# Every second panel of the last up GEMM as three fp32r passes, with low parts made by accumulating transfers

## The reference

```python
def conv_ffn(h, w_up, conv_w, conv_b, w_down, rows):
    u = h @ w_up
    if rows is None:
        u = dwconv1d(u, conv_w[1], conv_b)
    else:
        u = dwconv2d_grid(u, conv_w, conv_b, rows)
    a, g = jnp.split(u, 2, axis=-1)
    return (jax.nn.silu(g) * a) @ w_down
```

## Time and profile before

| | before |
|---|---|
| median of 3 runs | 2967.87 us |
| the profiled execution, its own time | 2972.56 us |
| its span | 2970.5 us |
| TensorE matmul busy | 2742.2 us (92%) |
| VectorE busy | 1932.8 us (65%) |
| ScalarE busy | 1088.4 us (37%) |
| GpSimd busy | 183.0 us (6%) |
| mean granted TensorE clock | 0.973 |

### The profile page before, as it was taken

The page is one execution under the profiler, slowest core; times in us unless marked ns, Lnnn a source line. Parts: engine busy times, 40 slices in busy tenths (PEclk is TensorE's granted clock), DMA queues, the critical chain, the costliest instruction groups (busy, mean ns, idle before and its releaser), DMA issues.

```text
span 2970.5 us, 48700 instructions
## 1 busy us (share of the span) xinstructions
PE 2742.2 (92%) x18394; PEld 2327.1 (78%) x18394; DVE 1932.8 (65%) x3303; ACT 1088.4 (37%) x1387; POOL 183.0 (6%) x85
## 2 busy tenths in 40 slices
PE   3999998999999998999989958999999899889998
PEld 3998977899999887899967844687744777668887
DVE  6776665677777765466756373577786676664881
ACT  2434432443542424154463542333300644442211
POOL 0000000000000000000022300244300000000000
PEclk9999999999999999999999979999999999999999
DMA  8775734577675543446412010122277221113441
GB/s 305 271 286 217 267 114 165 211 278 283 216 273 218 213 169 115 158 141 227 183 57 74 30 64 29 67 89 99 106 264 288 73 73 69 57 57 122 149 166 73
DMA packets 105950, 469.13 MB, mean 158 GB/s; under 512 B 7004, under 2 KB 56744, under 8 KB 57896
## 3 DMA queue, kind: packets, MB, share of 16 engines
q1 hardware_dynamic: 105768, 466.67, 43.3%
HBM read 465.58 MB, written 1.06 MB: 157 GB/s over the span
## 4 chain that ended last, share of the span: by engine, by line
PE 35%; DVE 10%; DVEq 7%; ACT 3%; issue 3%; DMA 1%; ACTq 1%; SPq 0%
PE accs L826 6%; DVEq L2818 4%; PE accs L687 4%; PE accs L688 4%; PE accs L689 4%; PE accs L672 4%; DVE arena L2795 3%; PE accs L1215 2%; PE accs L1216 2%; PE accs L1217 2%; DMA arena<-wc 1%; PE accs L1348 1%; ACT arena L76 1%; PE mix L1272 1%; DVE arena L2103 1%
## 5 line engine op out<-in xcount | busy, mean ns | idle before, releaser
L687 PE MATMUL accs<-normed_r,arena_r 128*128 128x256 f32 (+2 forms) x1864 | 586.4, 315 | 14.6 <-DVEq L2148 6.3
L689 PE MATMUL accs<-normed_r,panel_r 128*128 128x256 f32 (+2 forms) x1872 | 585.7, 313 | 0.0
L688 PE MATMUL accs<-arena_r 128*128 128x256 f32 x2069 | 584.5, 282 | 0.0
L86 DVE TENSOR_TENSOR panel_r<-panel,arena_r 128x1024 fp32r<-128x1024 f32 (+1 forms) x295 | 387.2, 1312 | 162.4 <-ACTq L1468 117.1
L1467 ACT ACTIVATE arena_r<-panel 128x1024 fp32r<-128x1024 f32 (+1 forms) x292 | 330.4, 1132 | 330.4 <-DMA panel<-w 140.8
L687 PEld LDWEIGHTS accs<-normed_r,arena_r 128*128 128x128 f32 (+1 forms) x1864 | 350.9, 188 | 51.8 <-issue 12.7
L688 PEld LDWEIGHTS accs<-arena_r 128*128 128x128 f32 x2069 | 389.3, 188 | 1.2 <-issue 0.2
L689 PEld LDWEIGHTS accs<-normed_r,panel_r 128*128 128x128 f32 (+1 forms) x1872 | 351.1, 188 | 24.2 <-issue 1.0
L672 PE MATMUL accs<-normed,panel 128*128 128x256 f32 x1536 | 344.8, 384 | 6.8 <-ACTq L475 3.0
L2795 DVE SCALAR_TENSOR_TENSOR arena<-accs,vectors,arena 128x189 f32<-128x189 f32 (+2 forms) x704 | 279.5, 428 | 96.9 <-issue 67.0
L672 PEld LDWEIGHTS accs<-normed,panel 128*128 128x128 f32 x1536 | 292.1, 192 | 54.3 <-issue 4.6
(11 more groups left out here) (406 smaller groups left out, 4705.3 us busy)
## 6 DMA issues: line engine op xcount, KB each, us to landing
panel<-w SPq DMA_DIRECT2D x250, 1024.0 KB, 4.9
panel<-w SPq DMA_DIRECT2D x48, 1408.0 KB, 8.0
cond_panel<-wc SPq DMA_DIRECT2D x57, 1024.0 KB, 6.2
normed<-wc SPq DMA_DIRECT2D x43, 1024.0 KB, 6.4
arena<-wc SPq DMA_DIRECT2D x19, 1024.0 KB, 5.0
residual<-xs SPq DMA_DIRECT2D x2, 1024.0 KB, 9.6
residual<-wc SPq DMA_DIRECT2D x1, 1024.0 KB, 13.0
residual<-crows SPq DMA_DIRECT2D x2, 512.0 KB, 9.2
```

The costliest lines, as they stand in the source:

```text
L86: i = self.eng.tensor_tensor(*a, **k)
L687: pe.matmul(out, hi[:, k, 0:m], src_hi(k), start=clear and k == 0, stop=False, skip_group_check=True)
L688: pe.matmul(out, hi[:, k, 0:m], src_lo(k), start=False, stop=False, skip_group_check=True)
L689: mm = pe.matmul(out, lo[:, k, 0:m], src_hi(k), start=False, stop=last and k == n - 1, skip_group_check=True)
```

## The change

The panels 3, 5, 7, ..., 21 of `up1` (ten of 22) are done in three fp32r passes; the other twelve stay float32. Panel i of the ten has the number m = (i-3)/2. For each:

- ScalarE, after its work on panel i-2, waits for the load of panel i, rounds the whole panel (128x2048) into `last_w[m % 2]`, and then writes the negative of the rounded panel over the panel itself in its slot.
- GpSimd, before its multiplication of the pair of panels i-3 and i-2, waits for both and issues a DMA that adds the panel from HBM once more onto the slot (`accum_op=ALU.add`). What is left there is the weights minus their high part.
- TensorE does 32 matmuls with the high part (on the high and the low part of the input), waits for that DMA, and does 16 with the low part.

Once at the stage's start ScalarE rounds the input `H` (two ACTIVATEs of 128x1024) into `last_hi`, and VectorE makes `last_lo` (two subtractions of 128x1024). TensorE, ScalarE and GpSimd run this stage unrolled in place of their loops; VectorE and SyncE keep theirs. Two semaphore increments are dropped to make room: ScalarE's wait on `lb_diff` near the kernel's start becomes a wait for the third weighing of the head (`cond_done` at 3), and `ml_decays`, for which nothing waited, goes.

```diff
+        last_hi, last_lo = H_r[:, :, 0:T], cond_slot1_r[:, :, :]
+        last_w = [sums_r[:, 2 * i:2 * i + 2, :].rearrange("p a (k c) -> p (a k) c", k=4) for i in range(2)]
...
+            def last_up(i, n):
+
+                g = G["up1"]
+                if i < 3 or i % 2 == 0:
+                    features(g, i // 4, i % 4, lambda k: H[:, k, lat], T, n)
+                    return
+                m = (i - 3) // 2
+                b = acc_open(g, i // 4, i % 4)
+                w, rest = last_w[m % 2], slots_r[(g.p0 + i) % SLOTS]
+                if m == 0:
+                    pe.wait_ge(S("low_made"), 2 * g.s0 + 1)
+                pe.wait_ge(S("up_parts"), 2 * m + 2)
+                for j in range(2):
+                    out = acc[b][:, j * T:j * T + T]
+                    for k in range(KD):
+                        pe.matmul(out, w[:, k, j * P:j * P + P], last_hi[:, k, :], start=(j == 0 and k == 0), stop=False, skip_group_check=True)
+                        pe.matmul(out, w[:, k, j * P:j * P + P], last_lo[:, k, :], start=False, stop=False, skip_group_check=True)
+                pe.wait_ge(up_low[m % 2], 16 * (m // 2 + 1))
+                for j in range(2):
+                    for k in range(KD):
+                        mm = pe.matmul(acc[b][:, j * T:j * T + T], rest[:, k * PANEL + j * P:k * PANEL + j * P + P], last_hi[:, k, :],
+                                       start=False, stop=(k == KD - 1), skip_group_check=True)
+                mm.then_inc(ready[b], 1)
...
-                    groups(pe, G["up1"], lambda it, u, n=rms: features(G["up1"], it, u, lambda k: H[:, k, sel], ntok, n), peel=True)
+                    for i in range(G["up1"].n):
+                        last_up(i, rms)
...
                 if u % 2 == 1:
+                    i = 4 * it + u + 2
+                    if i < g.n:
+                        m = (i - 3) // 2
+                        pool.wait_ge(S("up_parts"), 2 * m + 3)
+                        pool.dma_start(slots_r[(g.p0 + i) % SLOTS][:, 0:KD * PANEL], w8[g.row0 + i:g.row0 + i + 1, :, :].rearrange("a p n -> p (a n)"),
+                                       accum_op=ALU.add).then_inc(up_low[m % 2], 16)
                     par = u // 2
                     pool.wait_ge(S("up_silu"), it * 2 + (11 + par + 1))
...
-            groups(pool, g, gated)
+            for i in range(g.n):
+                gated(i // 4, i % 4)
...
                     if u % 2 == 1 and not (isinstance(it, int) and it == 0 and par == 0):
                         silu(1 - par, it * 2 + (11 * l + par))
 
-                groups(act, g, body, peel=True)
+                    i = 4 * it + u + 2
+                    if l == 1 and i % 2 == 1 and i < g.n:
+                        s = (g.p0 + i) % SLOTS
+                        act.wait_ge(landed[s], 16 * ((g.p0 + i) // SLOTS + 1))
+                        full = slots[s][:, 0:KD * PANEL].rearrange("p (k c) -> p k c", k=KD)
+                        rest = slots_r[s][:, 0:KD * PANEL].rearrange("p (k c) -> p k c", k=KD)
+                        act.activation(last_w[(i - 3) // 2 % 2], full, ACT.Copy).then_inc(S("up_parts"), 1)
+                        act.activation(rest, full, ACT.Copy, scale=-1.0).then_inc(S("up_parts"), 1)
+
+                if l == 0:
+                    groups(act, g, body, peel=True)
+                else:
+                    for k in range(0, KD, 4):
+                        last = act.activation(last_hi[:, k:k + 4, :], H[:, k:k + 4, lat], ACT.Copy)
+                    last.then_inc(S("up_parts"), 1)
+                    for i in range(g.n):
+                        body(i // 4, i % 4)
...
-            act.wait_ge(S("lb_diff"), 1)
+            act.wait_ge(S("cond_done"), 3)
...
+                if l == 1:
+                    dve.wait_ge(S("up_parts"), 1)
+                    for k in range(0, KD, 4):
+                        dve.tensor_tensor(last_lo[:, k:k + 4, :], H[:, k:k + 4, lat], last_hi[:, k:k + 4, :], ALU.subtract)
+                    dve.drain().then_inc(S("low_made"), 1)
                 groups(dve, g, body, peel=True)
```

More of the change, by code:

```diff
@@ L444, in program @@
         first_used = sem("first_half_used")
+        up_low = [sem(f"up_low_landed{i}") for i in range(2)]
         cond_landed = [sem(f"cond_landed{i}") for i in range(2)]
@@ L2571, in decays @@
                     if p == 3:
-                        dve.drain().then_inc(S("ml_decays"), 1)
+                        dve.drain()
                 def normalise(n, tok):
@@ L2865, in _ @@
                 dve.tensor_tensor(small[:, 4 * i:4 * i + 4], lb[i], small[:, 8:12], ALU.subtract)
-            dve.drain().then_inc(S("lb_diff"), 1)
+            dve.drain()
             for i in range(2, 5):
```

## The result

The changed kernel takes 3030.3 us (median of 4 runs, 3026.38 to 3038.12) against 2965.11 us for the kernel before beside it. The ratio is 1.0208, 95% interval 1.019 to 1.0226: slower by 62 us by the ratio, 65 by the medians. The forecast was 3018 us with a range of 2981 to 3064. Medians are told over all runs of a kernel and ratios over the fast ones alone, since a few runs of experiments 1, 8 and 10 and of the kernel beside them were 500 to 9000 us longer.

The account below looks back on a forecast made before the run. VectorE was taken to bound the kernel, TensorE nearly level; the change adds a serial loop through the transfer. Loop +43.2 us and clock +7.5 us on the median 2967.9 gave 3018 us, range 2981 to 3064.

Parts of the forecast that it names:

- VectorE is the slower: In `up1` before the change, VectorE takes 7.84 us a panel against TensorE's 6.91, so VectorE sets the pace.
- neither form can give more than 1 us back: Serial loop or VectorE's pace: whatever the transfer takes, `up1` gets at most 1 us shorter.
- TensorE's 12 us: Ten split panels of `up1`, each 1.20 us shorter on TensorE, 12.0 us by TensorE alone.
- The floor: Panel 21's preparation follows a SiLU waiting for VectorE's panel 17: at least L - 1.0 us over before.
- 8.58 + L: Serial round per split panel of `up1`: two evacuations, SiLU, two copies, transfer, 16 low matmuls, start of evacuation.
- L: Accumulating transfer, from the last copy until TensorE may go on: 4.9 + 2.4 + 2.4 = 9.7 us, upper end 12.4.
- 43.2 + 7.5 = 50.7: Slowdown in us: 43.2 from the serial loop at L = 9.7, 7.5 from the lower TensorE clock.
- The clock: TensorE's waits for the transfer lower its clock: 1.5 us a split panel, 15 in all, half taken, +7.5 us.
- The small parts: Input rounding, GpSimd's queue, SyncE's loads, the early wait, unrolled TensorE code: nothing, up to 2 us for code fetch.
- third one: The forecast's own case, L = 8 to 11: 2994 to 3039 us for the loop, up to 15 more for clock; 41%.
- 10 L - 53.8: Change in the start of `down1`, in us, by the serial loop of ten rounds; +43.2 at L = 9.7.
- rival 1: VectorE stays the bound in `up1`, transfer costs a plain load, L up to about 6: +3.9 us, 2972; 9%.

Follow-up runs that it names:

- experiment 1: Changed kernel with GpSimd's transfers plainly writing the panel instead of adding, low part left out: 2978.26 us, ratio 1.0027.
- 8: Changed kernel with copies and transfer one panel earlier, and GpSimd's transfer issued ahead of the multiplication: 2975.36 us, ratio 1.0016.
- 10: Changed kernel with the low part made by two GpSimd subtractions, without ScalarE's negated copy and the transfer: 2972.75 us, ratio 1.0.
- experiment 3: Changed kernel without GpSimd's ten transfers, TensorE waiting for ScalarE's second copy instead, low part left out: 2971.58 us, ratio 1.0001.
- 7: Kernel before the change with VectorE's loop of this stage written out: 2967.22 us, ratio 0.999.
- 11: Changed kernel with the low part made by GpSimd subtractions and VectorE's loop of this stage written out: 2957.29 us, ratio 0.9961.
- 12: Changed kernel with each accumulating transfer cut to the panel's first 512 KB, half of the low part left out: 2987.66 us, ratio 1.0065.
- experiment 2: Changed kernel with SyncE loading only the first 128 KB of even panels 4 to 18: 3014.86 us, ratio 1.0138.
- experiment 4: Changed kernel with 16 small float32 filler matmuls on TensorE before its wait for the transfer: 3026.78 us, ratio 1.018.
- 9: Changed kernel with copies and transfer one panel earlier, transfer ahead of GpSimd's multiplication, VectorE's loop written out: 2977.14 us, ratio 1.0021.

## Why the prediction was right

**The bound.** "VectorE is the slower" and "neither form can give more than 1 us back": held. Without a transfer the time is that of the kernel before (experiment 3, ratio 1.0001), and only with VectorE's pace changed too do TensorE's 12 us appear (7, 10, 11). The floor itself was not quite right: it left out that the high matmuls of panel 21 wait for the first copy, and without any transfer the stage is 1.9 us longer where it said 1.0 shorter (experiment 3).

**The loop.** The form, one serial round of 8.58 + L for each pair, is what the chain of waits shows line by line. The mean round of 20.26 us comes apart into L 10.50, low matmuls 3.62, 0.03 until the evacuation starts, 5.97 for evacuations, SiLU and copies, and 0.14 for one table load in nine rounds. The forecast had 1.90, 0.29 and 6.39 for the middle three.

**The steepness**, ten rounds for each microsecond of L: held, with the low matmuls beside L. Against the changed kernel the stage is shorter by

| | stage, us | 10 x mean L | 10 x mean low matmuls |
|---|---|---|---|
| half transfer (12) | 36.8 | 29.5 | 7.2 |
| short loads (2) | 13.1 | 9.8 | 3.3 |
| filler (4) | 3.6 | -3.3 | 6.9 |
| plain transfer (1) | 47.1 | 40.2 | 9.6 |

Only in the last is the sum 2.7 us too large; there ScalarE's SiLU waits for VectorE in two rounds, 2.2 and 0.7 us. The floor begins to show.

**The size.** The stage grew by 60.9 us, forecast were 43.2 + 7.5 = 50.7. The terms of L and of the low matmuls, told below, were too small by 7.1 and 9.6 us; the shorter work on ScalarE (5.97 for 6.39, and 5.25 for 5.59 in the first round) and the shorter start of the evacuation (0.03 for 0.29) gave back 4.1 and 2.6.

**L**, taken as 9.7: measured 10.4. Its parts were less right than their sum. A plain transfer in company was 4.9 + 2.4 = 7.3; experiment 1 has a mean L of 6.4, and the company in it costs 1.4, if it costs a plain transfer what it costs an adding one in experiment 2. The adding was "a second megabyte is read", 2.4 us; it measured 4.0. Errors of -0.9 and +1.6 partly cancelled, and that the sum came so near is luck.

**The clock.** I took half of its 15 us, but the granted clock fell behind all ten waits. The 16 low matmuls took 3.61 us at the mean against 2.07 in experiment 3, 1.5 us in each of ten panels. They were also 0.17 us longer at full clock than the 1.90 of the sum.

**The small parts** at nothing: VectorE's first tap came 1.3 us after ScalarE's first evacuation as before, so the rounding of the input stayed hidden. TensorE's unrolled code left no gap ahead of `down1`, whose first matmul follows the low matmuls of panel 21 at once.

**The rivals.** The third one's "2994 to 3039 for the loop, up to 15 more for the clock" counts the clock twice: by 10 L - 53.8 the loop alone ends at 3024 for L = 11, and 3039 has the 15 us in it. The measured 3030 us with L = 10.4 lie in it with the clock counted once. Of the signs, the rounds were somewhat longer than foretold (18.3 to 23.2 us for 18 to 20), TensorE's waits 3.3 to 8.7 us for 4 to 7, and `down1` started at 2942.7 us for 2925.

**The rules.** By the Trainium skill, "DMA: Bandwidth & Descriptors", "Anatomy of one DMA — SWDGE (gpsimd) path", a panel's transfer from GpSimd would take an estimated 4.4 us; the plain one landed in 5.3 beside other loads and the adding one in 9.3, so rival 1, on which it landed, fell. The two source reads that the Trainium skill, "Collectives: The Full Stack", "The bandwidth ceiling: the fold count and why AG ≠ RS ≠ AR", gives for the adding step of a ReduceScatter led to an estimate of 6.8 us; it points the right way, and 9.3 us is more.

## What to carry to other kernels

Before making one engine's work shorter, look at which engine holds the bank or buffer that opens its last piece; the chain of waits named VectorE's loop here, and the gain needed both edits. When a new step is put between two others, write down the loop that it closes over all queues, GpSimd's own included, and multiply its latency by the number of rounds; move it ahead by a panel only together with everything queued before it. A transfer that adds is a poor substitute for a subtraction on an idle engine: 9.3 us against 4.7 for the same megabyte, and a second copy on ScalarE saved.

## What the runs showed of the hardware

- A DMA that adds from GpSimd landed in 9.3 us for 1024 KB and 6.6 for 512 KB (medians), a plain one from GpSimd in 5.3, and one from SyncE in 4.9. Its issue held GpSimd for 0.88 us, that of a plain one for 0.59.
- The time of another load moves the landing by about 2 us: 10.5 to 11.8 us with SyncE's load 0.81 us or less behind or ahead of the adding transfer, 8.8 to 10.0 with the load 0.97 us or more behind (twenty transfers, changed kernel and experiment 4). The load was slowed as well: 7.3 to 11.2 us in the changed kernel beside an adding transfer, against 4.9; nothing waited for it.
- GpSimd's drain waits for its own outstanding transfer: 6.5 us behind a multiplication of 1.26, ending as the transfer landed (experiments 8 and 9, 18 drains). This was not expected, and it puts a transfer's latency in front of any work that GpSimd signals after a drain. That another form of signal would avoid it was not tried.
- VectorE's eight taps on two halves take 6.7 to 6.9 us a panel written out and 7.7 or more in the hardware loop, where 0.17 us or more of idle time stand before each pair of instructions (kernel before). Which part of the loop causes it was not tried.
